# A two-block transformer kernel on one core: the orders of four queues are moved, two score products are joined, and a bias becomes one product

## The reference, cut to what matters

```python
def attention_mixer(h, positions, w_in, b_in, sinks, w_out, b_out):
    proj = h @ w_in + b_in
    q, k, v, z = jnp.split(proj, ...)
    q = partial_rope(q, positions); k = partial_rope(k, positions)
    o = sliding_window_gqa(q, k, v, sinks)
    return (o * jax.nn.silu(z)) @ w_out + b_out

def hgrn2_mixer(h, lower_bound, w_in, gnorm_w, w_out):
    proj = h @ w_in
    q, f, i, z = jnp.split(proj, ...)
    q = jax.nn.silu(q)                      # 8 heads, key dim 128
    log_f = jnp.logaddexp(jnp.log(lb), jnp.log1p(-lb) + jax.nn.log_sigmoid(f))
    k = -jnp.expm1(log_f)
    o = chunked_gated_recurrence(q, k, i, log_f)
    o = o * rsqrt(mean(o * o) + eps) * gnorm_w
    return (o * jax.nn.silu(z)) @ w_out

# the recurrence: S_t = f_t * S_(t-1) + k_t v_t ; o_t = q_t S_t, so that
# score[t, s] = sum over the key dim of q_t * (f_(s+1) ... f_t) * k_s   for s <= t
```

## Time and profile before

| | us |
|---|---|
| median of three runs | 911.25 |
| the profiled execution's own time | 911.09 |
| its span | 909.4 |
| TensorE busy in the span | 892.2 |
| VectorE busy | 654.7 |
| ScalarE busy | 486.2 |
| GpSimd busy | 47.2 |

### The profile page before, as it was taken

The page is one execution under the profiler, slowest core; times in us unless marked ns, Lnnn a source line. Parts: engine busy times, 40 slices in busy tenths (PEclk is TensorE's granted clock), DMA queues, the critical chain, the costliest instruction groups (busy, mean ns, idle before and its releaser), DMA issues.

```text
span 909.4 us, 15736 instructions
## 1 busy us (share of the span) xinstructions
PE 892.2 (98%) x6260; PEld 807.1 (89%) x6260; DVE 654.7 (72%) x903; ACT 486.2 (53%) x704; POOL 47.2 (5%) x86
## 2 busy tenths in 40 slices
PE   8999999999999999999999999999999999999997
PEld 7999889999999899888899999998778779988986
DVE  5756558877777886666598768778677776798684
ACT  6555647654654673655565455455636567521252
POOL 2900000000000010000100000000100001000000
PEclk9999999999999999999999999999999999999999
DMA  7553325555455355323264554654443234532221
GB/s 278 194 173 139 140 93 177 217 191 205 159 195 204 139 180 186 139 94 139 94 249 151 226 185 144 225 186 169 162 142 136 95 139 162 186 139 93 94 93 47
DMA packets 21801, 144.51 MB, mean 159 GB/s; under 512 B 2816, under 2 KB 2832, under 8 KB 5104
## 3 DMA queue, kind: packets, MB, share of 16 engines
q1 hardware_dynamic: 20160, 139.47, 43.0%
q0 software_dynamic: 1296, 4.19, 1.6%
q10 hardware_dynamic: 288, 0.04, 0.0%
HBM read 142.64 MB, written 1.05 MB: 158 GB/s over the span
## 4 chain that ended last, share of the span: by engine, by line
PE 89%; DVE 5%; ACT 2%; issue 1%; DMA 1%; POOL 0%; DVEq 0%; SPq 0%; POOLq 0%; ACTq 0%
PE psC L1739 20%; PE psC L1740 19%; PE psC L1741 19%; PE psD L1739 4%; PE psD L1740 4%; PE psD L1741 4%; PE psD L2451 2%; PE psC L1837 2%; PE psC L1839 2%; PE psC L1846 2%; DVE w_lo L970 1%; PE psD L2079 1%; PE psD L2056 1%; PE psD L2068 1%; PE psD L2109 1%
## 5 line engine op out<-in xcount | busy, mean ns | idle before, releaser
L970 DVE TENSOR_TENSOR w_lo<-raw,w_hi 128x2048 fp32r<-128x2048 f32 x125 | 285.5, 2287 | 61.0 <-ACT w_hi L491 60.3
L491 ACT ACTIVATE w_hi<-raw 128x2048 fp32r<-128x2048 f32 x125 | 238.6, 1913 | 81.3 <-PE psC L1741 70.0
L1739 PE MATMUL psC<-xT_hi,w_hi 128*128 128x256 f32 x960 | 273.3, 285 | 0.0
L1740 PE MATMUL psC<-xT_lo,w_hi 128*128 128x256 f32 x960 | 271.6, 283 | 0.0
L1741 PE MATMUL psC<-xT_hi,w_lo 128*128 128x256 f32 x960 | 271.5, 283 | 0.0
L1739 PEld LDWEIGHTS psC<-xT_hi,w_hi 128*128 128x128 f32 x960 | 184.0, 192 | 2.5 <-issue 1.9
L1740 PEld LDWEIGHTS psC<-xT_lo,w_hi 128*128 128x128 f32 x960 | 184.1, 192 | 0.6
L1741 PEld LDWEIGHTS psC<-xT_hi,w_lo 128*128 128x128 f32 x960 | 184.1, 192 | 0.0
L610 ACT ACTIVATE arena<-arena,pv 128x256 f32<-128x256 f32 x88 | 45.8, 591 | 95.1 <-DVE arena L1141 95.1
L1151 DVE SCALAR_TENSOR_TENSOR arena<-arena,pv 128x254 f32<-128x254 f32 (+1 forms) x176 | 75.4, 480 | 20.9 <-ACT arena L610 16.6
L1739 PE MATMUL psD<-w_hi,oT_hi 128*128 128x512 f32 x208 | 81.5, 392 | 0.6 <-DVE w_lo L970 0.6
(11 more groups left out here) (312 smaller groups left out, 1345.3 us busy)
## 6 DMA issues: line engine op xcount, KB each, us to landing
raw<-stream SPq DMA_DIRECT2D x130, 1024.0 KB, 4.8
gbc<-post_g POOLq DMA_DIRECT2D x6, 512.0 KB, 4.3
h<-x_in SPq DMA_DIRECT2D x2, 512.0 KB, 5.6
raw<-stream SPq DMA_DIRECT2D x4, 256.0 KB, 7.4
out<-h SPq DMA_DIRECT2D x4, 256.0 KB, 2.0
arena<-b_in POOLq DMA_DIRECT2D x1, 640.0 KB, 4.9
pv<-pvec POOLq DMA_DIRECT2D x1, 176.0 KB, 8.9
arena<-wf POOLq DMA_DIRECT2D x2, 64.0 KB, 2.8
```

Source lines behind the costliest of these rows:

```text
L491: nc.scalar.activation(w_hi[:, slot, :], raw[:, raw_slot, :], ACT.Copy).then_inc(hi_done, 1)
L970: V.tensor_tensor(w_lo[:, slot, :], raw[:, raw_slot, :], w_hi[:, slot, :].bitcast(F32), ALU.subtract).then_inc(lo_done, 1)
L1739: MM(out, lhs[0], rhs[0], start=start, stop=False, skip_group_check=True)
L1740: MM(out, lhs[0], rhs[1], start=False, stop=False, skip_group_check=True)
```

## The change

Parts, in the order of the program:

1. The beginning: both halves of x are loaded before any quarter of unit 0; `pos` moves from ScalarE's queue to the end of SP's first loads; ScalarE makes quarter 0 of `w_hi` behind the first two `xT_hi`.
2. Last MLP chunk: VectorE splits the last unit before `gate_lo`.
3. Narrow turn: ScalarE splits U+1 before two squares of the norm; VectorE splits U+1 before the row means; the spread scales are taken later; the bias parts are made behind the split of U+5.
4. Window: ScalarE makes the first gate before a split, VectorE splits U+7 behind the first gated output.
5. Output bias: `b_out` is loaded into 33 rows; row 0 holds the high part and row 32 the low part; a matrix with -1 in rows 0 and 32 and 0 between multiplies both in one matmul per bank.
6. Recurrence: the silu goes to another buffer (`X[1]`), so that plain and decayed queries lie 2048 columns apart, and one matmul per tile of 256 columns gives the diagonal and level 1 (`first_level`, two halves of 8 tiles); two masked copies per half take them out (`pick_first`). `block_totals` moves ahead of the second query chunk; levels 2 to 7, `cross` and `outputs` move one part back in `AFTER`.
7. Tail: `out_scaled` stands before the split of the last `rec_z` unit; the last 512 columns of h are updated and stored in two pieces.

```diff
-            sp.dma_start(h[:, 0, :], x_in[0, 0:P, :]).then_inc(x_loaded[0], 16)
-            quarter(0)
-            sp.dma_start(h[:, 1, :], x_in[0, P:2 * P, :]).then_inc(x_loaded[1], 16)
-            for q in range(1, 4):
+            for tt in range(TT):
+                sp.dma_start(h[:, tt, :], x_in[0, tt * P:tt * P + P, :]).then_inc(x_loaded[tt], 16)
+            for q in range(4):
                 quarter(q)
             for u in range(EARLY, RAW):
                 sp.dma_start(raw[:, u, :], stream[u]).then_inc(raw_loaded[u], 16)
+            sp.dma_start(pos_i[:, :], pos).then_inc(pos_loaded, 16)
...
-            pool.dma_start(bout_row, b_out.partition_broadcast(1)).then_inc(bias_loaded, 16)
+            pool.dma_start(bout_row, b_out.partition_broadcast(33)).then_inc(bias_loaded, 16)
...
             pre(4, "at_pre")
+            split_to(U0["at_kv"] + 2)
             for c in range(2):
                 pre_square(4, 1, c)
-            split_to(U0["at_kv"] + 3)
+            split_to(U0["at_z"] + 1)
             act.wait_ge(bias_loaded, 32)
-            nc.scalar.activation(bout_hi, bout_row, ACT.Copy, scale=-1.0).then_inc(bias_split, 1)
+            nc.scalar.activation(bout, bout_row, ACT.Copy, scale=-1.0).then_inc(bias_split, 1)
...
-                    gate_lo(j, j % 2)
                     if j == NJ - 1:
                         split_to(u0 + 3 * NJ)
+                    gate_lo(j, j % 2)
...
                 gate_rows(0)
-                split_to(u0 + 3)
                 normalize(1, 1)
                 gate_made(0)
                 gated(0)
+                split_to(u0 + 3)
...
-                        for part, first in ((bout_hi, True), (bout_lo, False)):
-                            MM(o_bank(4, tt, c), neg_ones_r[0:1, :], part[:, 512 * c:512 * c + 512], start=first, stop=False,
-                               skip_group_check=True)
+                        MM(o_bank(4, tt, c), two_rows, bout[:, 512 * c:512 * c + 512], start=True, stop=False, skip_group_check=True)
...
+            def first_level(half):
+
+                pe.wait_ge(rec["ready"], half + 1)
+                pe.wait_ge(rec["decayed"], half + 1)
+                if half:
+                    pe.wait_ge(rec["picked"], 1)
+                for i in range(8):
+                    t = 8 * half + i
+                    queries_ = arena[:, 4096 + P * t:8192 + P * t].rearrange("p (two n) -> p two n", two=2)[:, :, 0:P]
+                    ins = MM(psD[:, i // 2, 256 * (i % 2):256 * (i % 2) + 256].rearrange("p (two n) -> p two n", two=2), kk_tiles[t],
+                             queries_, start=(i % 2 == 0), stop=True, skip_group_check=True)
+                ins.then_inc(rec["level"], 1)
...
-            AFTER = {1: [level_diagonal], 2: [lambda: level(1)], 3: [lambda: level(2)], 4: [lambda: level(3)], 5: [lambda: level(4)],
-                     6: [lambda: level(5)], 7: [lambda: level(6)], 8: [lambda: level(7)], 9: [cross],
-                     10: [lambda: outputs(0), lambda: outputs(1)], 15: [lambda: turn_outputs(0)]}
+            AFTER = {1: [lambda: first_level(0)], 2: [lambda: first_level(1)], 4: [lambda: level(2)], 5: [lambda: level(3)],
+                     6: [lambda: level(4)], 7: [lambda: level(5)], 8: [lambda: level(6)], 9: [lambda: level(7)], 10: [cross],
+                     11: [lambda: outputs(0), lambda: outputs(1)], 15: [lambda: turn_outputs(0)]}
...
-            split_to(ro)
             out_scaled(0)
             out_scaled(1)
+            split_to(ro)
```

More of the change, by code:

```diff
@@ L209, in build @@
         ffn = [{n: sem(f"ffn{i}_{n}") for n in ("scaled", "centre", "tap1", "gate", "up", "gelu", "g", "g_hi", "g_lo")} for i in range(2)]
-        rec = {n: sem(f"rec_{n}") for n in ("bound", "bounds", "sigmoid", "silu", "cleared", "ready", "decayed", "total", "level", "cross", "crossed",
+        rec = {n: sem(f"rec_{n}") for n in ("bound", "bounds", "sigmoid", "silu", "cleared", "ready", "decayed", "total", "level", "same", "cross", "crossed",
                                             "picked", "gate", "o", "osq", "sums", "omean", "oscale", "scaled", "gated", "turned", "ohi", "olo")}
@@ L554, in pre @@
                     ins.then_inc(xT_hi_done, 1)
-                    if n == 0 and b:
+                    if n == 0:
                         early_quarter(0, b)
@@ L1098, in post @@
                                                ALU.add).then_inc(signal, 1)
+                    update(1, 1)
                 else:
                     update(1, 0)
-                update(1, 1)
+                    dve.wait_ge(norm_gain, 2 * TT * i + 4)
+                    for lo, hi, signal in ((512, 768, last_rows_new), (768, 1024, h_new)):
+                        V.scalar_tensor_tensor(h[:, 1, lo:hi], hn[:, 1, lo:hi], st[:, n, 4, 1:2], h[:, 1, lo:hi], ALU.mult,
+                                               ALU.add).then_inc(signal, 1)
             def chunk_wait(name, c):
@@ L1610, in _, with pick_first @@
             tiles = sc_diag.rearrange("p (g t) -> p g t", t=P)
-            def pick_diagonal():
-                dve.wait_ge(consts_pool, N_CONSTS)
-                dve.wait_ge(rec["level"], 1)
-                dve.wait_ge(rec["cleared"], 1)
-                for half in range(2):
-                    ins = V.copy_predicated(tiles[:, 8 * half:8 * half + 8, :], mask_level[:, 0, :].unsqueeze(1).to_broadcast([P, 8, P]),
-                                            psD_rows[:, half, :].rearrange("p (g t) -> p g t", t=P))
-                ins.then_inc(rec["picked"], 1)
+            def pick_first(half):
+                if half == 0:
+                    dve.wait_ge(consts_pool, N_CONSTS)
+                    dve.wait_ge(rec["cleared"], 1)
+                dve.wait_ge(rec["level"], half + 1)
+                got = psD[:, :, :].rearrange("p k n -> p (k n)").rearrange("p (g two n) -> p g two n", two=2, n=P)
+                out_ = tiles[:, 8 * half:8 * half + 8, :]
+                V.copy_predicated(out_, mask_level[:, 0, :].unsqueeze(1).to_broadcast([P, 8, P]),
+                                  got[:, :, 1, :]).then_inc(rec["same"], 1)
+                dve.wait_ge(rec["same"], half + 1)
+                out_, got = (a.rearrange("p g (b two) -> p g b two", two=2)[:, :, :, 1] for a in (out_, got[:, :, 0, :]))
+                mask = mask_level[:, 1, :].rearrange("p (b two) -> p b two", two=2)[:, :, 1]
+                V.copy_predicated(out_, mask.unsqueeze(1).to_broadcast([P, 8, 64]), got).then_inc(rec["picked"], 1)
             def pick(n):
@@ L1649, in _ @@
             split_to(ri + 3)
-            pick_diagonal()
-            block_totals()
+            pick_first(0)
             decay(1)
-            pick(1)
+            pick_first(1)
             split_to(ri + 4)
@@ L2432, in _ @@
             kk_tiles, query_tiles = ([a[:, P * i:P * i + P] for i in range(TT * REC_H)] for a in (kk, X[0]))
-            def level_diagonal():
-                pe.wait_ge(rec["ready"], 2)
-                pe.wait_ge(rec["silu"], 2)
-                for i in range(TT * REC_H):
-                    ins = MM(psD[:, i // 4, P * (i % 4):P * (i % 4) + P], kk_tiles[i], qT[:, i // 2, P * (i % 2):P * (i % 2) + P],
-                             start=(i % 4 == 0), stop=True, skip_group_check=True)
+            def first_level(half):
[8 more added lines that the diff above has]
+                             queries_, start=(i % 2 == 0), stop=True, skip_group_check=True)
                 ins.then_inc(rec["level"], 1)
@@ L2446, in level @@
                 pe.wait_ge(rec["decayed"], n + 1)
-                pe.wait_ge(rec["picked"], max(n - 1, 1))
+                pe.wait_ge(rec["picked"], max(n - 1, 2))
                 for i in range(TT * REC_H):
```

39 lines of the change are left out of this document (25 added, 14 removed).

## The result

The changed kernel takes 916.57 us (median of 14 runs), the kernel before 911.48 us in the same session. Two of the 14 were disturbed (1080.56 and 3825.97 us); the other twelve have a median of 915.5 us and give the ratio 1.0045, 95% interval 1.0032 to 1.0057. It is slower by 4 to 5 us, outside my range. The twelve fall into two groups of six, 913.0 to 914.6 us at a mean granted clock of 0.996 to 0.998, and 916.5 to 918.4 us at 0.992 or 0.993. The profiled execution is of the second: 917.88 us (span 916.0), 6.8 more than the profiled one of before.

The account below looks back on a forecast made before the run. TensorE, busy 98% of the span, was taken to bound the kernel. The terms -1.65 - 0.8 + 0.7 - 1.5 - 0.95 + 2.0 + 2.6 gave +0.4: 911.5 us profiled, 911.7 beside the median; range 908.2 to 913.7.

Parts of the forecast that it names:

- beginning: Start of the kernel: the 2.1 us wait for x vanishes, less 0.5; gain 1.65 us, ends 1.0 and 2.1.
- last MLP chunks: Last MLP chunk: the split no longer waits for ScalarE's high part; gain 0.8 us, ends 0.4 and 0.9.
- narrow turn, its waits: Narrow turn: U+1's wait goes, but U+3 waits for b_out; TensorE at 662.9, a loss of 0.7 us.
- window: Window attention: the whole wait for the first gated output goes; gain 1.5 us, at least 1.0.
- output bias: Output bias: four of eight products go, each about 0.24 us; gain 0.95 us, ends 0.8 and 1.1.
- first scores, its waits: Recurrence: TensorE waits 3.0 us for the pick before the second half; net 2.0 us lost, ends 1.3 and 2.6.
- tail: Tail: outputs stands one part (2.83 us) later, scalings save 0.2; 2.6 us lost, ends 1.8 and 2.8.
- B: Narrow turn: landing time of b_out, taken as 657.7 between 655.3 and 659.2; TensorE starts U+3 at B + 5.2.
- rivals: Four alternatives: loads do not collide 0.17; recurrence or tail cheaper 0.15; bias load worse 0.13; beginning does nothing 0.05.
- the estimate by the Trainium skill's rule of whole packets in turn: Narrow turn: loads alternate, all 3.4 MB before the last lands; B = 658.3, a loss of 1.3 instead of 0.7.
- My first rival: Narrow turn: POOL's loads get through beside SP's, B near 655.3; 2.4 us better, 909.3; chance 0.17.

Follow-up runs that it names:

- start_only: Kernel before with the edit of the beginning alone (x ahead of quarter 0, positions later, quarter 0's high part later): 909.46 us, ratio 0.9978.
- bias_twice: Changed kernel with narrow-turn loads earlier, totals behind the first half-pick and recurrence as before; each of four 33-row bias products issued twice: 903.98 us against 903.01.
- after: The changed kernel itself, with all parts of the change, against the kernel before: 916.57 us median, 917.88 us profiled.
- runs with zeros: Changed kernel with 24 and 16 products of zeros on TensorE ahead of U+3 and of first_level's second half: 912.82 us.
- both edits: Changed kernel with narrow-turn loads issued ahead of the power and block totals behind the first half of the first pick: 905.51 us, ratio 0.9933.
- before_totals: Kernel before with only the six block totals moved ahead of the diagonal's pick: 918.75 us, ratio 1.0080.
- totals_back: Changed kernel with the six block totals moved behind the first half of the first pick: 912.09 us, ratio 1.0008.
- both_tail: Changed kernel with narrow-turn loads earlier and totals behind the first half-pick, plus level 2 and all that follows one part earlier: 908.67 us.

## Why the prediction was wrong

By its own steps, profiled against profiled, and from start to start of the products:

| step | predicted | measured | from |
|---|---|---|---|
| beginning | -1.65 | -1.3 (alone -1.8) | first product at 9.81; start_only |
| last MLP chunks | -0.8 | -1.1 | both waits gone; TensorE is 2.4 earlier behind them |
| narrow turn, its waits | +0.7 | +1.8 | wait 4.4, U+1's 1.1 gone |
| window | -1.5 | -1.6 (alone -1.6) | wait gone |
| output bias | -0.95 | -0.9 (bias_twice 1.0) | TensorE from the first bias product to the first scores |
| first scores, its waits | +2.0 | +2.2 | wait 2.8, ended by the pick |
| tail | +2.6 | +2.1 | 0.4 and 1.6 |
| half clock behind the waits | no such term | 2.3 + 3.0 = +5.3 | windows at 0.50 |

The column measured sums to 6.5 of the 6.8 found. Without its last row it would be 1.2, against my 0.4: 912.3, inside the range. The narrow turn's 1.8: the program arrives there 2.4 us earlier than before (1.3 + 1.1), so U+3's 661.59 answers to 664.0, beside the 662.17 of the earlier trace rows.

The last row is that of the profiled execution, one of the longer group. By medians the term is about half of it: after lies 2.7 us above the runs with zeros (915.5 and 912.8), and both edits win 2.7 more than their waits. Four of after's twelve runs, at 0.997 or 0.998, even lie inside my range. So which executions get the half clock decides by how much the forecast is missed, and that is chance.

**The step that failed** is that a wait of TensorE was priced at its own length: "TensorE starts U+3 at max(659.5, B + 5.2)" and "Net: 3.0 - 0.8 - 0.2 = 2.0 lost". The product behind the wait was taken at the duration it has in rows where TensorE came to it busy. In the trace of before no product behind a wait was slow: its longest wait of TensorE inside the run of work was 1.4 us, and the 2.1 us for x stands in the start. But the idle end of the program (908.30:909.40 at 0.50, above) showed that the clock falls when TensorE stands, so "full speed throughout" was true only as long as it worked. None of the rivals spoke of the clock, though the forecast itself made the two longest waits of the program. Zeros, both edits, and the runs of one program at two clocks show the term; before_totals shows it without any of the change.

**A smaller miss:** B, the whole of the narrow turn's 1.1. TensorE did start U+3 at B + 5.2 (656.42 and 661.59). But I took 657.7 between 655.3 and 659.2; counted from POOL's first issue that is 9.0 us, and it was 10.1 here and 1.5 more in totals_back, where b_out took 10.5 us from its own issue in place of 9.0. It was the upper end (10.5) that should have been taken, since SP's two loads cover the stretch: the estimate by the Trainium skill's rule of whole packets in turn (DMA: Bandwidth & Descriptors, Queues, rings and completion order), which I set aside, came nearer, by 0.6 us. My first rival (the loads don't collide) needed them to be issued earlier, and then it came true.

**Smaller still:** the scores were reckoned with waits of "0.5 and 0.3 us" before; the earlier trace rows show one wait, 0.32 us idle and 0.5 from start to start. With it alone the step is 3.0 - 0.5 - 0.2 = 2.3, beside the 2.2 measured. The last MLP chunks won 1.1, more than the upper end of 0.9; the tail lost 2.1, within its ends.

**Right**, with their mechanism: the beginning, the MLPs, the window, the bias, the place and releaser of all three new waits. Why start_only wins 1.8 us, where its profiled execution wins 1.5 and that of the whole change 1.3 at the first product, isn't shown. A clue is the clock: runs of the kernel before have means from 0.995 to 1.000 (910.3 to 912.9 us), and without the wait of 2.1 us for x none of 11 is below 0.998.

## What to carry to other kernels

A wait of TensorE has two prices: its length, and half of the work that falls into the stretch at 1.2 GHz that may follow. In the profiles here waits up to 1.7 us in the run of work brought none. Waits of 2.4 to 2.9 us brought it in many executions but not in all and then added 1.7 to 3.3 us. Those of 3.5 to 5.8 us brought it in every profile and added 1.5 to 4.7; the longest added least, since its half clock lay mostly inside the wait. So by these rows several short waits are cheaper than one long one of the same sum, and an edit that gathers them is to be priced with the clock. Look at mean clock and PE's busy time first when fewer products take longer.

Where a wait can't be moved, let TensorE do products of zeros into a bank that is being summed (5.1 us here). Better, take the cause away: issue a load as soon as its buffer is free, not behind the result that happened to stand ahead of it, and keep work that nobody waits for behind the pick that TensorE waits for.

## What the runs showed of the hardware

- The length of the half-clock stretch varied for one and the same wait of 2.8 us: none, 3.2 and 6.7 us; behind 3.5 us it was 10. It can begin inside the wait (659.7) or some 2 us behind it (811.6, in both_tail). Behind the last product of the program, with TensorE idle for good, it began 4.4 us later in before, and 2.2 to 5.2 us later over the 13 profiles. Why one execution gets it and the next doesn't stays open; nothing here was varied for it.
- A load of 132 KB on POOL's queue landed 9.0 to 10.5 us after its issue beside SP's units (four profiles), and 5.5 to 6.3 us where it was issued earlier (five).
- At the beginning of before_totals products of 256 columns took 0.41 us until 14.5 us, in place of 0.28, while the granted clock reads 1.00: there the column alone doesn't tell.
- Four products of 512 columns with 33 rows took 1.19 us, as four with a single row did.
